# A two-block transformer on one core: the group norm's products moved to GpSimd, second-tile attention units scaled by two per-partition values, sigmoid gates inverted once

## The reference, cut to what matters

```python
y_a = chunked_spatial_gating(z_a, ...)
# rwkv7_time_mix, after the recurrence gave ys, per token and head of 64 channels:
mu_y = jnp.mean(y, axis=-1, keepdims=True)
var_y = jnp.mean(jnp.square(y - mu_y), axis=-1, keepdims=True)
y = ((y - mu_y) * lax.rsqrt(var_y + GN_EPS)).reshape(Bn, S, B_WIDTH)
y = y * gn_g + gn_b
y_b = (y + bonus) * g                     # bonus = sum(r * k * r_k) * v
# nsa_attention: sigmoid gates g_t, three softmax attentions over the same queries
o = g_t[..., 0:1] * o_c + g_t[..., 1:2] * o_s + g_t[..., 2:3] * o_w   # compressed, selected, windowed
h = h + jnp.concatenate([y_a, y_b, y_c], axis=-1) @ w_out[i]
```

## Time and profile before

| | us |
|---|---|
| median of three runs | 2137.06 |
| span of the profiled execution, first to last instruction | 2134.8 |
| TensorE busy | 2014.6 (94%) |
| VectorE busy | 748.1 (35%) |
| ScalarE busy | 594.7 (28%) |
| GpSimd busy | 29.4 (1%) |

### The profile page before, as it was taken

One profiled execution on the slowest core, in us unless ns is written; L12 is line 12 of the kernel. 1 busy time (PEld: TensorE's weight loads), 2 busy tenths in 40 slices (PEclk: granted clock), 3 DMA queues, 4 the chain that ended last, 5 costly groups with the idle time before them and its releaser, 6 DMA issues.

```text
span 2134.8 us, 38508 instructions
## 1 busy us (share of the span) xinstructions
PE 2014.6 (94%) x17136; PEld 1254.8 (59%) x17136; DVE 748.1 (35%) x1339; ACT 594.7 (28%) x975; POOL 29.4 (1%) x40
## 2 busy tenths in 40 slices
PE   9999999978988879999999999999999999999996
PEld 7778884322432237877888887845556554344445
DVE  8775662110100116786444677610001000000016
ACT  6555541000100015465334755400000000000005
POOL 1000000000000000100000000000000000000000
PEclk9999999999999999999999999999999999999999
DMA  9754467999999997264555551389999999999991
GB/s 222 204 153 144 152 231 296 421 421 421 421 421 422 421 408 226 83 168 158 177 179 196 163 174 42 133 302 404 410 412 395 365 403 409 412 408 408 412 408 66
DMA packets 239198, 622.94 MB, mean 292 GB/s; under 512 B 35496, under 2 KB 120360, under 8 KB 201648
## 3 DMA queue, kind: packets, MB, share of 16 engines
q1 hardware_dynamic: 233872, 611.87, 76.5%
q10 hardware_dynamic: 4544, 6.42, 0.8%
q0 software_dynamic: 608, 2.10, 0.2%
HBM read 614.43 MB, written 3.81 MB: 290 GB/s over the span
## 4 chain that ended last, share of the span: by engine, by line
PE 74%; DMA 15%; DVE 6%; ACT 3%; issue 1%; SPq 0%; POOL 0%; DVEq 0%; ACTq 0%; POOLq 0%
PE ps L2798 21%; PE ps L2815 11%; DMA ring<-in_w_down 5%; PE ps L659 5%; PE ps L661 5%; PE ps L660 5%; PE ps L2502 4%; DMA ring<-in_w_gate 4%; DMA ring<-in_w_up 3%; PE ps L669 2%; PE ps L670 2%; PE ps L673 2%; PE ps L2517 2%; DMA arena<-in_w_gate 1%; DMA arena<-in_w_down 1%
## 5 line engine op out<-in xcount | busy, mean ns | idle before, releaser
L2798 PE MATMUL ps<-ring,arena 128*32 128x512 f32 (+1 forms) x3936 | 395.2, 557 | 0.0
L699 DVE TENSOR_TENSOR ring_parts<-ring,high_parts 128x2048 fp32r<-128x2048 f32 (+2 forms) x118 | 264.1, 2245 | 107.9 <-ACT high_parts L695 107.0
L2798 PEld LDWEIGHTS ps<-ring,arena 128*32 128x32 f32 x3936 | 147.8, 110 | 230.4 <-issue 222.6
L3008 DVE TENSOR_TENSOR arena<-ps,arena 128x768 f32<-128x768 f32 (+1 forms) x24 | 21.4, 891 | 600.8 <-ACT arena L2913 537.5
L695 ACT CAST high_parts<-ring 128x2048 fp32r<-128x2048 f32 (+2 forms) x118 | 219.3, 1863 | 39.3 <-PE ps L661 29.1
L661 PE MATMUL ps<-high_parts,arena_parts 128*128 128x512 f32 (+1 forms) x508 | 200.0, 394 | 0.0
L659 PE MATMUL ps<-high_parts,hT_parts 128*128 128x512 f32 (+1 forms) x480 | 194.9, 406 | 0.0
L2502 PE MATMUL ps<-ring,arena 128*64 128x512 f32 x664 | 167.0, 596 | 24.9 <-DMA ring<-in_w_up 13.8
L660 PE MATMUL ps<-ring_parts,hT_parts 128*128 128x512 f32 (+1 forms) x480 | 188.4, 393 | 0.0
L2815 PE MATMUL ps<-ring,arena 128*32 128x256 f32 x3168 | 176.1, 379 | 0.0
L2913 ACT ACTIVATE arena<-ps,arena 128x256 f32<-128x256 f32 (+1 forms) x72 | 27.6, 454 | 521.0 <-PE ps L2798 521.0
(11 more groups left out here) (631 smaller groups left out, 2452.5 us busy)
## 6 DMA issues: line engine op xcount, KB each, us to landing
ring<-in_moe_w SPq DMA_DIRECT2D x220, 512.0 KB, 9.9
ring<-in_moe_w SPq DMA_DIRECT2D x66, 1024.0 KB, 12.6
ring<-in_w_gate SPq DMA_DIRECT2D x42, 1024.0 KB, 26.7
ring<-in_w_down SPq DMA_DIRECT2D x42, 1024.0 KB, 27.0
ring<-in_w_up SPq DMA_DIRECT2D x41, 1024.0 KB, 26.8
ring<-in_moe_w SPq DMA_DIRECT2D x108, 384.0 KB, 8.0
ring<-in_w_in SPq DMA_DIRECT2D x104, 256.0 KB, 4.6
arena<-in_w_up SPq DMA_DIRECT2D x23, 1024.0 KB, 26.1
```

Of the source, the lines that this page charges most:

```text
L699: dve.tensor_tensor(low_flat(p), raw_flat(p), f32(high_flat(p)), ALU.subtract).then_inc(split, 1)
L2798: mm = pe.matmul(dst, x_rows, w[:, :, s * n:(s + 1) * n], start=(c == 0), stop=(c == KC - 1), skip_group_check=True)
```

## The change

- The square (L3714), the product with the gain (L3718), the product with the reciprocal (L3721) and the last sum (L3722) leave VectorE for GpSimd (`pool_`). The sum of squares and its scaling (L3715, L3716) move to VectorE's `chain(1)`, the reciprocal (L3720) to its `chain(5)`. The bias term lies in another buffer (`w_shift`).
- The square root (L3632) moves on ScalarE from ahead of the units to the end of round 4, behind `turned(4)`.
- The gates' exponential (L3956) moves up to stand between the copies L3951 and L3953. VectorE inverts 1 + exp(-gate logit) once (a reciprocal of 128x48), and each unit multiplies by it.
- Units of tile 1 multiply each head's 256 probabilities by two values per partition in one instruction, two instructions a unit, instead of L4058 and L4061.
- TensorE and ScalarE get waits for GpSimd's results; the upper halves of the first two pieces of the output weights swap places.

```diff
@@ highs
-            group_out[l].high = highs(20864, 18816, 16768, 7728)
+            group_out[l].high = highs(18816, 20864, 16768, 7728)
@@ rwkv, act_
                 act_aside(act, "turned")
-                act.wait_ge(*at("rw_var"))
-                act.activation(small[:, 24:32], small[:, 16:24], ACT.Sqrt).then_inc(sig("rw_sd"), 1)
@@ rwkv, pool_
+                flat2 = lambda a: a.rearrange("p t n -> p (t n)")
+                pool.wait_ge(*at("rw_cent"))
+                pool.tensor_tensor(flat2(w_km), flat2(w_y), flat2(w_y), ALU.mult).then_inc(sig("rw_sq"), 1)
+                pool.tensor_tensor(flat2(w_y), flat2(w_y), flat2(w_gain), ALU.mult).then_inc(sig("rw_yg"), 1)
+                pool.wait_ge(*at("rw_rs"))
+                pool.wait_ge(*at("rw_yg"))
+                pool.tensor_tensor(heads(w_y), heads(w_y), per_head(small[:, 0:8]), ALU.mult).then_inc(sig("rw_yr"), 1)
+                pool.wait_ge(*at("rw_yr"))
+                pool.tensor_tensor(ycat[:, :, AW:AW + BW], w_y, w_shift, ALU.add).then_inc(sig("rw_yn"), 1)
@@ rwkv, dve_
-                dve.wait_ge(*at("rw_cent"))
-                vstep(dve, dve.tensor_tensor(f(w_km), f(w_y), f(w_y), ALU.mult))
-                vstep(dve, dve.tensor_reduce(small[:, 0:8], w_km.rearrange("p t (h n) -> p (t h) n", h=BH), AX, ALU.add))
-                dve.tensor_scalar(small[:, 16:24], small[:, 0:8], 1.0 / HD, GN_EPS, ALU.mult, ALU.add).then_inc(sig("rw_var"), 1)
                 dve_aside(dve, LEV)
-                dve.tensor_tensor(f(w_y), f(w_y), f(w_gain), ALU.mult)
-                dve.wait_ge(*at("rw_sd"))
-                vstep(dve, dve.reciprocal(small[:, 0:8], small[:, 24:32]))
-                vstep(dve, dve.tensor_tensor(heads(w_y), heads(w_y), per_head(small[:, 0:8]), ALU.mult))
-                dve.tensor_tensor(ycat[:, :, AW:AW + BW], w_y, w_bias, ALU.add)
@@ nsa, pe_, chain(9)
                             pe.wait_ge(*at("nsa_ablo", 1))
+                            pe.wait_ge(*at("rw_yn"))
@@ nsa, act_aside "turned"
+                    act.activation(n_gate, z[:, :, CGT:ZW], ACT.Exp, scale=-1.0).then_inc(sig("nsa_gate"), 1)
                     act.wait_ge(*at("nsa_q"))
@@ nsa, act_
-                act.activation(n_gate, z[:, :, CGT:ZW], ACT.Exp, scale=-1.0).then_inc(sig("nsa_gate"), 1)
...
+                    if u == 6:
+                        act.wait_ge(*at("rw_yg"))
+                    if u == 9:
+                        act.wait_ge(*at("rw_yn"))
...
                     turned(u)
+                    if u == 4:
+                        act.wait_ge(*at("rw_var"))
+                        act.activation(small[:, 24:32], small[:, 16:24], ACT.Sqrt).then_inc(sig("rw_sd"), 1)
@@ nsa, dve_
                 vstep(dve, dve.tensor_scalar(n_gate, n_gate, 1.0, None, ALU.add))
+                vstep(dve, dve.reciprocal(n_gate, n_gate))
...
-                    vstep(dve, dve.tensor_tensor(n_rd[:, q], n_den[:, q], gates, ALU.mult))
-                    vstep(dve, dve.reciprocal(n_rd[:, q], n_rd[:, q]))
+                    vstep(dve, dve.reciprocal(n_rd[:, q], n_den[:, q]))
                     p = n_sm[u % 4].rearrange("p (j n) -> p j n", j=n)
+                    if t:
+                        for j in range(n):
+                            k = 3 * (h0 + j) + 1 + br
+                            ins = dve.tensor_scalar(p[:, j], p[:, j], n_rd[:, 4 * u + j:4 * u + j + 1], n_gate[:, t, k:k + 1], ALU.mult, ALU.mult)
+                        ins.then_inc(sig("nsa_scaled"), 1)
+                        return
+                    vstep(dve, dve.tensor_tensor(n_rd[:, q], n_rd[:, q], gates, ALU.mult))
@@ nsa, dve_, chain(1)
+                        dve.wait_ge(*at("rw_sq"))
+                        vstep(dve, dve.tensor_reduce(small[:, 0:8], w_km.rearrange("p t (h n) -> p (t h) n", h=BH), AX, ALU.add))
+                        dve.tensor_scalar(small[:, 16:24], small[:, 0:8], 1.0 / HD, GN_EPS, ALU.mult, ALU.add).then_inc(sig("rw_var"), 1)
@@ nsa, dve_, chain(5)
+                        dve.wait_ge(*at("rw_sd"))
+                        dve.reciprocal(small[:, 0:8], small[:, 24:32]).then_inc(sig("rw_rs"), 1)
                         dve.wait_ge(*at("nsa_cexp"))
```

More of the change, by code:

```diff
@@ L257, in emit @@
                                   "rw_tt5": 2, "rw_tt6": 2, "rw_Uv": 1, "rw_H1": 1, "rw_U1": 1,
[1 row of a table removed]
-        count_steps("rw_pool", {"rw_lm": 5})
[1 row of a table added]
+        count_steps("rw_pool", {"rw_lm": 5, "rw_sq": 1, "rw_yg": 1, "rw_yr": 1, "rw_yn": 1})
         count_steps("nsa_tensor", {"nsa_blkT": 1, "nsa_k": 1, "nsa_qr": 1, "nsa_q": 1, "nsa_hidT": 1, "nsa_cmp": 1,
                                    "nsa_sc": 1, "nsa_pcturned": 1, "nsa_abT": 2})
-        count_steps("nsa_scalar", {"nsa_pairs": 1, "nsa_rest": 1, "nsa_k2": 1, "nsa_kT": 1, "nsa_qrT": 1, "nsa_qT": 1,
-                                   "nsa_gate": 1, "nsa_gexp": 1, "nsa_cexp": 1, "nsa_out": 4})
+        count_steps("nsa_scalar", {"nsa_pairs": 1, "nsa_rest": 1, "nsa_k2": 1, "nsa_kT": 1, "nsa_qrT": 1, "nsa_gate": 1,
+                                   "nsa_qT": 1, "nsa_gexp": 1, "nsa_cexp": 1, "nsa_out": 4})
         count_steps("nsa_vector", {"nsa_krot": 1, "nsa_rot": 1, "nsa_blk": 1, "nsa_row": 1, "nsa_gpoly": 1, "nsa_hid": 1,
@@ L3205, in emit @@
         w_y, w_gain, w_bias = w_lw, w_a, w_B
+        w_shift = hT_flat[:, 2 * 512:3 * 512].rearrange("p (t n) -> p t n", t=NT)
         w_ss, w_most, w_root = [small[:, a:a + 8] for a in (40, 48, 56)]
@@ L3662, in bonus @@
                     if k == 4:
-                        return dve.tensor_tensor(w_bias, w_bias, row(6), ALU.add)
-                    return dve.tensor_tensor(f(w_bias), f(w_bias), f(w_g), ALU.mult)
+                        return dve.tensor_tensor(w_shift, w_bias, row(6), ALU.add)
+                    return dve.tensor_tensor(f(w_shift), f(w_shift), f(w_g), ALU.mult)
                 dve.wait_ge(*at("rw_g"))
@@ L3742, in emit @@
         n_mx, n_den, n_rd = [MN.take(12 * 4) for _ in range(3)]
+        n_qT = MN.take(CH // 2, S)
         n_gate = MN.take(NT, 3 * CH)
-        n_qT = MN.take(CH // 2, S)
-        assert w_end <= MN.at
+        assert w_end <= MN.at - NT * 3 * CH
         n_qrT = MN.take(CH // 2, S)
@@ L4107, in chain @@
                         gates = n_gate.rearrange("p t (h b) -> p t h b", b=3)[:, :, :, 0]
-                        vstep(dve, dve.tensor_tensor(r, r, gates, ALU.mult))
-                        vstep(dve, dve.reciprocal(n_cs[:, 1, :], n_cs[:, 0, :]))
+                        vstep(dve, dve.reciprocal(n_cs[:, 0, :], n_cs[:, 0, :]))
+                        vstep(dve, dve.tensor_tensor(n_cs[:, 1, :].rearrange("p (t h) -> p t h", t=NT), r, gates, ALU.mult))
                         vstep(dve, dve.tensor_tensor(sc16, sc16, n_cs[:, 1, :].unsqueeze(2).to_broadcast([P, 16, 16]), ALU.mult))
```

## The result

The changed kernel takes 2142.43 us, the median of nine runs (2141.97 to 2145.05), the kernel before 2137.41 (nine runs beside them, 2135.85 to 2140.22). The ratio is 1.0023, 95% interval 1.0014 to 1.0032: slower by 5.0 us. The forecast was 2144.0, slower, in a range of 2136 to 2148.5.

What follows compares the result with a forecast made beforehand. TensorE, busy 33.9 of 36 us in each unit stage, was taken as the bound. Per stage -1.60 (start), +2.86 (loads) and +2.2 (clock) made +3.5, +6.9 in both: 2137.06 became 2144.0 us, range 2136 to 2148.5.

Steps and rivals of the forecast that it cites:

- Start of the units: Before `scores(2)` and `turn(0)`, TensorE's idle times of 0.65 and 0.95 us go: 1.60 us gained a stage.
- Rounds 1 to 4 and the two-value products: TensorE is bound by its own queue, so VectorE's 0 to 0.25 us saved a unit was costed at nothing.
- The 0.35 us a product: In tile 1 units, estimated VectorE time for one 128x256 product with a per-partition value from SBUF: 0.35 us.
- The loads on the path: Two table loads around the root in round 4: TensorE waits 3.2 us before `chain(6)`, starting it 1.26 us later than before.
- The walk from the copy to the compressed scores' exponential: ScalarE's steps from `turned(4)` through load, root, load and unit 6's exponentials to that exponential: 4.39 us.
- the 2.8 us for two drains: At the root's two table switches, the skill page's cost implied 2.8 us more a stage than the forecast's walk.
- The clock: Behind the 3.2 us wait TensorE's clock falls to its lower level: 2.2 us a stage, bounds 0 and 3.4.
- rival 1: The root stalls TensorE at `chain(6)` but the clock holds: 2139.6 us; chance 0.13.
- GpSimd, nothing: GpSimd's four 128x512 products, at the units' start and behind the root, hold up VectorE only under cover: cost 0.
- The cover named: Spare transposes at the start and VectorE's wait for ScalarE behind the root hide GpSimd's hold-ups; without it up to 1.3 us a stage.
- Sum: All terms over both unit stages: +3.5 us a stage, +6.9 us in two, giving 2144.0 us.
- rival 4: The unexplained idle time with fallen clock at 1276 us moves: gone 2139.5 us, a second one 2148.5; chance 0.12.

Runs made afterwards that it cites:

- experiment 5: The changed kernel run once more with no edit; 2143.04 us, ratio 1.0025 to the kernel before.
- prods: Kernel before with only the gates' reciprocal made once, the two-value products and two small steps of `chain(5)` reordered; 2138.00 us, ratio 1.0001.
- gapspares: The changed kernel with 28 more spare transposes on TensorE ahead of `chain(6)`, filling its wait; 2141.20 us, ratio 1.0013.
- u3: First follow-up: the changed kernel with the square root one round earlier, behind turned(3); 2137.56 us, ratio 0.9999.
- copysq: The changed kernel with a copy in place of the square root, so no table is loaded; 2136.31 us, ratio 0.9992.
- u3r7: The changed kernel with the root at round 3 and VectorE's reciprocal of it moved from `chain(5)` to `chain(7)`; 2135.75 us, ratio 0.9987.
- b_nospare: Kernel before without the 5 spare transposes in each of rounds 1 to 11; 2134.51 us, ratio 0.9978.
- n_again: Second run of u3r7 without the 5 spare transposes in each of rounds 1 to 11; 2129.67 us, ratio 0.9961.

## Why the forecast was right, step by step

- **Start of the units, -1.60 a stage: right, a little small.** Both idle times went. Without a clock fall `turn(0)` starts 1.8 us earlier (914.72 in experiment 5, 916.55 before, both stages starting at 908.05): I had added up durations where the rows start closer together.
- **Rounds 1 to 4 and the two-value products, nothing: right** (prods 1.0001). The 0.35 us a product was 0.37.
- **The loads on the path: right, and the deciding step.** Expected idle 3.2 us, measured 3.21 in every layer of both executions. The forecast had `chain(6)` 1.26 us later; without the fall ahead it is 25.92 - 24.85 = 1.07, the same 0.2 us less. The walk from the copy to the compressed scores' exponential was right to 0.03 us, and the 2.8 us for two drains, which the forecast set beside it, didn't come: the root starts 0.01 us behind its load and the next load 0.02 behind the root. Behind it 0.2 us more came back, so that a stage without falls is 47.88 - 47.03 = 0.85 us longer. gapspares, whose clock holds, shows the same 0.86 by stages and +0.13% by medians. u3 and copysq show that the loads are not the only thing late there: without them GpSimd's lock takes 1.70 - 0.55 = 1.15 us of the same place, as u3r7, with neither, waits 0.55.
- **The clock, +2.2 a stage: mechanism right, size too large.** A fall is 3.4 us long and costs 1.4 to 1.5 us: from `chain(6)` to the stage's end are 50.91 - 27.53 = 23.38 us with it and 47.88 - 25.92 = 21.96 without. In one layer of four it did not come, so over the two executions it is about 2.2 us in both stages, not 4.4; gapspares against after says 2.1 to 2.6, with intervals that overlap. The term took the middle of 1.7 and 3.4; the lower one less the part inside the wait would have been near. What the forecast held against rival 1, that no idle time over 3 us had left the clock alone, failed in that one layer.
- **GpSimd, nothing: right here, for the reason given** (VectorE was waiting for ScalarE anyway). The cover named was real: as soon as experiment 1 took the loads away, the bill of up to 1.3 us came, 1.15 us. So did the hold-up of the gates' addition at the start, 0.50 instead of 0.12 us in experiment 5; the spare transposes hid it, as foreseen.
- **Not foreseen:** a clock fall ahead of the units, 1.6 us a stage in the profiled execution. It stands in four of the 26 layers of all profiled executions, all four in kernels with the changed group norm (after, u3, u3r7; 20 layers). Two more layers have one in the first rounds (prods and b_nospare, made from the kernel before), and the second execution of after has none. What brings it is open.
- **Sum.** Forecast +6.9; profiled +6.6, by another mix: +0.85 and +1.4 (late fall) and +1.6 (early fall) a stage, -2.7 for the fall that is gone at 1276 (rival 4, in part), +1.5 in the tail. The nearness of the two is partly luck: the early falls and the tail, which the forecast had not, made up for the smaller price of the late fall and for what went at 1276; of the medians' +5.0, the lateness of `chain(6)` is 1.7 (stages) to 2.8 (gapspares' ratio), the clock behind it 2.1 to 2.6, and up to 1.2 us stay unassigned. The tail's longer idle time, 1.1 us in both executions, would be about that much; as it is absent in gapspares (4.32 us) and present in u3 (5.50), it isn't a part of the mechanism above.

## What to carry to other kernels

Two table loads of 1.28 us are cheap where ScalarE waits, and not behind the copy that the next round's exponentials and a side branch hang on: place such a step by who is late behind it, here one round earlier. Work moved to GpSimd frees VectorE only while VectorE isn't running or about to run a product with two operands in SBUF or with per-partition values; if a short pair of products must run beside it, one long product that starts first is the better form. An idle TensorE queue filled with spare work hides the lateness of others; before tuning those others, take the filling away and see who waits.

## What the runs showed of the hardware that I had not expected

- A product with per-partition values and a single SBUF operand of 128x256 can be held up by GpSimd as two-operand ones are: 1.68 to 1.74 us for two instead of 0.74, in u3r7 and in n_again. The gates' addition of 128x48 too took 0.50 us beside GpSimd's first pair and 0.12 where it came after it.
- The same wait of 3.21 us was followed by a clock of 1.00 in one layer of four and by 3.4 us at 1.2 GHz in three, and one of 1.70 us (u3) by such a fall in one layer of two. Ahead of the units (L3871), where no wait of the 14 us before was over 0.72 us, TensorE ran at 1.2 GHz in some executions and at 2.4 in others.
- GpSimd's operation on 128x512 took 1.04 us in the first of two in a row and 1.26 to 1.28 in the second, in every kernel with the change's group norm, where VectorE left it alone.
- 55 spare transposes less per layer came with 1.6 to 1.9 us less idle time in a part of the program that executes none of them, and that part was 3.6 us (from u3r7) to 4.5 us (from before) shorter. The idle time of L2783 in the tail, ended by "issue" too, is 5.46 to 5.53 us in after, its second execution, u3 and u3r7, 5.19 in copysq, and 4.3 to 4.4 us in before, prods, gapspares and all five executions without them. Neither idle time is explained.
